# A seventh place for expert pieces, an earlier expert order, and sums moved ahead of the last pair in a two-layer mixture-of-experts decoder kernel

## What is computed

```python
def _hier_moe(u, rg_w, rg_b, re_w, re_b, w1, w3, w2):
    g_prob = softmax(t @ rg_w + rg_b)             # 4 groups of 4 experts
    g_val, g_idx = lax.top_k(g_prob, 1)
    e_prob = softmax(logits of that group)
    e_val, e_idx = lax.top_k(e_prob, EXPERT_TOPK) # 2 experts of the group
    weights = g_val * e_val / sum(e_val)
    h1, h3 = t @ w1[e], t @ w3[e]                 # 16 experts, 1024 x 512 each
    act = silu(h1) * h3 * combine
    return sum over experts of act @ w2[e]        # 512 x 1024
```

## Time and profile before

| what | value |
|---|---|
| time, median of 3 runs | 1069.71 us (1064.26 to 1069.83) |
| the profiled execution, its own time | 1063.24 us |
| its span | 1061.4 us |
| granted TensorE clock, mean share | 0.967 |
| PE busy | 978.4 us (92%) |
| DVE, ACT, POOL busy | 324.4, 174.5, 40.0 us |
| moved by DMA | 316.22 MB, mean 298 GB/s |

### The profile page before, as it was taken

How to read it: one execution, slowest core, us unless ns; L and a number is a source line. 1 busy time by engine, 2 the same in 40 slices (tenths; PEclk the granted TensorE clock), 3 DMA queues, 4 the chain that set the end, 5 groups by cost and what they waited for, 6 DMA issues and landing times.

```text
span 1061.4 us, 13346 instructions
## 1 busy us (share of the span) xinstructions
PE 978.4 (92%) x5418; PEld 552.4 (52%) x5418; DVE 324.4 (31%) x823; ACT 174.5 (16%) x388; POOL 40.0 (4%) x68
## 2 busy tenths in 40 slices
PE   7999999999799989999889798999989998889796
PEld 3666655584464654444443256777664444434353
DVE  3141134216442361111110027738561111111025
ACT  2200000003230231111110012054231111001112
POOL 0000000002210000000002000000000000001000
PEclk9999999979889999999999899999999999999999
DMA  9845777828980529999999984214727999999971
GB/s 379 358 159 199 278 274 284 334 84 325 400 339 5 237 87 418 424 421 422 422 422 421 388 361 160 105 55 175 306 80 309 421 421 423 421 421 422 381 325 50
DMA packets 47622, 316.22 MB, mean 298 GB/s; under 512 B 5602, under 2 KB 6002, under 8 KB 12354
## 3 DMA queue, kind: packets, MB, share of 16 engines
q1 hardware_dynamic: 39456, 288.90, 67.4%
q0 software_dynamic: 6096, 22.30, 5.5%
q10 hardware_dynamic: 2002, 4.08, 1.0%
HBM read 303.84 MB, written 11.42 MB: 297 GB/s over the span
## 4 chain that ended last, share of the span: by engine, by line
PE 65%; DMA 28%; DVE 4%; issue 1%; SPq 1%; ACT 0%; DVEq 0%
PE banks L783 24%; DMA scr<-in_ew 19%; PE banks L1380 8%; DMA ring<-in_ew 6%; PE banks L860 4%; DMA ring<-in_w 3%; PE banks L1347 3%; PE banks L1396 3%; PE banks L1427 3%; PE banks L900 2%; PE banks L1445 1%; PE banks L847 1%; PE banks L1359 1%; PE banks L969 1%; PE banks L1467 1%; PE banks L792 1%
## 5 line engine op out<-in xcount | busy, mean ns | idle before, releaser
L1380 PE MATMUL banks<-scr 128*64 128x512 f32 x448 | 105.6, 621 | 24.7 <-DMA scr<-in_ew 24.4
L783 PE MATMUL banks<-uT,ring 128*128 128x320 f32 x448 | 123.0, 434 | 2.6 <-DVE uT L1629 2.6
L783 PEld LDWEIGHTS banks<-uT,ring 128*128 128x128 f32 x448 | 84.5, 190 | 41.6 <-issue 6.8
L1427 PE MATMUL banks<-ring,scr 128*64 128x512 f32 x448 | 99.7, 596 | 2.9 <-DMA ring<-in_ew 2.9
L1347 PEld LDWEIGHTS banks<-scr 128*128 128x128 f32 x768 | 88.1, 192 | 12.4 <-issue 12.4
L1347 PE MATMUL banks<-scr 128*128 128x128 f32 x768 | 92.1, 277 | 0.0
L1380 PE MATMUL banks<-ring,scr 128*64 128x512 f32 x384 | 84.5, 592 | 0.0
L1380 PEld LDWEIGHTS banks<-scr 128*64 128x64 f32 x448 | 31.9, 141 | 97.6 <-issue 57.6
L594 ACT ACTIVATE scr<-banks,mods 128x128 f32<-128x128 f32 x128 | 36.6, 368 | 204.8 <-PE banks L1347 204.8
L1427 PEld LDWEIGHTS banks<-ring,scr 128*64 128x64 f32 x448 | 30.8, 137 | 60.9 <-issue 54.8
L783 PE MATMUL banks<-ring,uT 128*128 128x512 f32 x128 | 57.0, 598 | 0.0
(11 more groups left out here) (378 smaller groups left out, 1024.7 us busy)
## 6 DMA issues: line engine op xcount, KB each, us to landing
ring<-in_ew SPq DMA_DIRECT2D x128, 1024.0 KB, 20.3
ring<-in_w SPq DMA_DIRECT2D x80, 1024.0 KB, 8.2
scr<-in_ew SPq DMA_DIRECT2D x64, 1024.0 KB, 23.3
yd<-scr POOLq DMA_DIRECT2D x12, 512.0 KB, 8.2
scr<-in_v POOLq DMA_DIRECT2D x16, 256.0 KB, 8.3
scr<-in_kT POOLq DMA_DIRECT2D x13, 256.0 KB, 7.8
out_hgrn<-scr SPq DMA_DIRECT2D x1, 2304.0 KB, 17.8
scr<-in_s POOLq DMA_DIRECT2D x1, 2048.0 KB, 9.5
```

The costliest lines, as they stand in the source:

```text
L783: last = mm(out, a, b, start=(first and i == 0), stop=(final and i == len(pairs) - 1))
L1380: ins = mm(ps[bank][SLOTS * x:SLOTS * x + SLOTS, :], xe[:, kk, SLOTS * x:SLOTS * x + SLOTS], wab[SLOT[n]][:, x, kk % 4, :], start=(kk == 0 ...
L1427: ins = mm(ps[5 + c][SLOTS * x:SLOTS * x + SLOTS, :], actT[:, f, SLOTS * x:SLOTS * x + SLOTS], wab2[SLOT[n]][:, x, f % 2, 512 * c:512 * c ...
```

## The change

1. A place 6 is made in the scratch tile at 10888 (`SPARE`). It lay under `yrows1` before; `yrows1` is now the tile `utok`, the token rows that the pairs' gathers read. So GpSimd waits, ahead of the six indirect DMAs, for the last pair's gather on TensorE (`xe_ps` 16). Some tiles of the dense path, which this input doesn't take, move too.
2. The expert pieces take seven places in a cycle of twelve: with a, b, c, d the ring tiles, a b 4 5 c d 6 a b 4 5 c. Pieces 7 to 11 follow their predecessor in a place at a distance of 7, pieces 12 to 16 at 5, pieces 17 and 18 at 12, and so on every twelve.
3. VectorE makes `order_i` first, with each exchange on 5 of the 8 rows (`swaps[:, TT:, :]`), then `over_i`, the weights, and the exchanges on the other 3 rows. `over_ready` is 2l+1 for the order and 2l+2 for `over_i`; SyncE waits for the first, the others for the second.
4. SyncE's pieces 2 to 5 of layer 0 also wait for `bias_ev` 4.
5. `add_first(6)` goes ahead of `hidden_last` with w1. It takes four products that need only columns 0 to 511 before it waits for ScalarE's copy.
6. In pairs 6 and 7 the second half of the w2 products has c outside, and each half of the columns has its own count, so that VectorE's copy can start when its half is done. `add_last` starts with products of that half. `SUM_ORDER` becomes 0 to 7.

```diff
-    order = further(order[0:2] + [4, 5] + order[2:4], MOE_PIECES)
+    def experts(order):
+        return order[0:2] + [4, 5] + order[2:4] + [6] + order[0:2] + [4, 5] + order[2:3]
+    order = [x for x in further(experts(order), MOE_PIECES) if x < RING]
...
+        SPARE = 10888
+        ring.append(scr[:, SPARE:SPARE + PIECE])
...
-        yrows1 = carve(11392, TT, D)
+        yrows1 = utok
...
-        SUM_ORDER = (0, 4, 1, 5, 2, 6, 3, 7)
+        SUM_ORDER = (0, 1, 2, 3, 4, 5, 6, 7)
...
-                            sp.wait_ge(sem("over_ready"), 2 * l + 2)
+                            sp.wait_ge(sem("over_ready"), 2 * l + 1)
...
-            experts(0, (("res0_ps", 1), ("kv_stored", 64)))
+            experts(0, (("res0_ps", 1), ("kv_stored", 64), ("bias_ev", 4)))
...
                     pool.wait_ge(sem(f"moved{b}"), 16 * stored(l, b, STORED))
+                pool.wait_ge(sem(f"xe_ps{l}"), 2 * NPAIR)
                 for t in ROWS_ORDER:
...
+                def steps(q, h):
+                    f = (2 * h, 2 * h + 1)
+                    if q >= STORED and h == 1:
+                        return [(i, c) for c in range(2) for i in f]
+                    return [(i, c) for i in f for c in range(2)]
...
                 def add_first(q):
                     pe.wait_ge(sem(f"ye_evv{l}"), q + 1)
+                    pe.wait_ge(sem(f"back_ev{l}"), 2)
+                    pe.wait_ge(sem(f"xe_ev{l}"), 2 * NPAIR)
+                    for i in range(4):
+                        prompt(i)
                     pe.wait_ge(sem(f"ye_eva{l}"), q + 1)
...
+                        if m == 4:
+                            pe.wait_ge(sem(f"ye_eva{l}"), q + 1)
...
+                add_first(NPAIR - 2)
                 hidden_last(0, 2, "h1_ps")
-                add_first(NPAIR - 2)
                 hidden_last(1, 3, "h3_ps")
...
+                places = ((NE - 2, MAX, swap), (NE - 1, MIN, swap2))
+                for h, best, oh in places:
+                    step(v.tensor_reduce(key_best, key[:, 2:NE], AX, best))
+                    step(ts(oh, key, key_best, None, EQ))
+                    exchange(swaps[:, TT:, :], h, oh)
+                cp(order_i[0:1, :], swaps[0:1, 2 * TT, 0:NE]).then_inc(sem("over_ready"), 1)
```

More of the change, by code:

```diff
@@ L340, in build @@
         yrows0 = [rows_flat[0][:, 0:D], rows_flat[0][:, D:2 * D], rows_flat[1][:, 0:D]]
[L341 removed]
+        yrows1 = utok
         cdiag = carve(704, 2, TT, P)
[L344 to L346 removed]
+        cb = carve(7424, 2, T)
+        sig = carve(8064, 2, T)
+        rms_all = carve(8704, T)
+        act = rows_flat[0].rearrange("p (a b c) -> p a b c", a=2, b=FT)
         def shift(s):
@@ L1305, in dense @@
                     give(mm(ps[7][:, 0:1], ones[:, :], ones[:, 0:1], start=True, stop=True))
+                mm(ps[7][:, 0:1], ones[:, :], ones[:, 0:1], start=True, stop=True).then_inc(sem(f"xe_ps{l}"), 2 * NPAIR - 3)
             def tokens(l, n):
@@ L1423, in outputs @@
                                 pe.wait_ge(sem(f"ye_eva{l}"), q)
[L1424 to L1430, removed]
+                        for f, c in steps(q, h):
+                            for x in range(2):
+                                ins = mm(ps[5 + c][SLOTS * x:SLOTS * x + SLOTS, :], actT[:, f, SLOTS * x:SLOTS * x + SLOTS],
+                                         wab2[SLOT[n]][:, x, f % 2, 512 * c:512 * c + 512],
+                                         start=(f == 0), stop=(f == FT - 1))
+                                give(ins, f"ye_ps{l}" if f == FT - 1 and (c == 1 or q >= STORED) and x == 1 else None)
                         used(n)
@@ L1440, in outputs_last @@
                             pe.wait_ge(sem(f"actT_ev{l}"), q + 1)
[L1441 to L1447, removed]
+                        for f, c in steps(q, h):
+                            w = wab2[SLOT[n]][:, :, f % 2, 512 * c:512 * c + 512]
+                            for b in range(4):
+                                ins = mm(ps[2 + c][BLOCK * b:BLOCK * b + BLOCK, :], actT[:, f, BLOCK * b:BLOCK * b + BLOCK],
+                                         of_block(w, b), start=(f == 0), stop=(f == FT - 1))
+                                give(ins, f"ye_ps{l}" if f == FT - 1 and b == 3 else None)
                         used(n)
@@ L1739, in slots, with exchange @@
                 counts = ps[6][:, TT * NE:TT * NE + NE]
+                def exchange(rows, h, oh):
+                    n = rows.shape[1]
+                    step(tt(change[:, 0:n, :], rows[:, :, h:h + 1].broadcast_to([P, n, NE]), rows[:, :, 0:NE], SUB))
+                    step(tt(change[:, 0:n, :], change[:, 0:n, :], over(oh, n, 1), MUL))
+                    v.tensor_reduce(total[:, 0:n].unsqueeze(2), change[:, 0:n, :], AX, ADD)
+                    step(tt(rows[:, :, 0:NE], rows[:, :, 0:NE], change[:, 0:n, :], ADD))
+                    step(tt(rows[:, :, h:h + 1], rows[:, :, h:h + 1], total[:, 0:n].unsqueeze(2), SUB))
+                ts(swaps[:, 2 * TT, 0:NE], const[:, K_IOTA:K_IOTA + NE], -NOWHERE, None, ADD)
+                step(stt(key, counts, float(NE), const[:, K_IOTA:K_IOTA + NE], MUL, ADD))
+                places = ((NE - 2, MAX, swap), (NE - 1, MIN, swap2))
[4 more added lines that the diff above has]
+                cp(order_i[0:1, :], swaps[0:1, 2 * TT, 0:NE]).then_inc(sem("over_ready"), 1)
                 v.tensor_reduce(n_most, counts[:, 2:NE], AX, MAX)
@@ L1749, in slots @@
                 step(v.tensor_reduce(n_over, fits[:, 32:36], AX, MAX))
+                ts(split_i[0:1, 0:1], n_most[0:1, :], float(SLOTS), None, ALU.is_le)
                 ts(over_i[0:1, 0:1], n_over[0:1, :], 0.0, None, MAX).then_inc(sem("over_ready"), 1)
[L1751 to L1753 removed]
                 combine(l)
[L1756 to L1764 removed]
+                for h, _, oh in places:
+                    exchange(swaps[:, 0:TT, :], h, oh)
                 ts(kept, slot[:, :, 0:NROWS], NOWHERE, None, GE)
```

66 lines of the change are left out of this document (33 added, 33 removed).

## The result

The changed kernel takes 1059.48 us at the median of 9 runs (1058.75 to 1062.91), the kernel before 1067.48 in 9 runs (1060.49 to 1070.01). The ratio is 0.9946, 95% interval 0.992 to 0.9971. It is faster, since the interval leaves out 1, by 5.8 us in 1067.5 by this ratio, which goes by the means (the medians lie 8.0 us apart), where 16 were forecast. The profiled execution took 1061.77 us, 1.5 less than the one before.

What follows compares the result with a forecast made beforehand. The two expert stages were taken as bound by the DMA queue, with a TensorE tail. Gains of 7.5 + 7.0 + 1.6 = 16.1 us gave 1047.1 from the profiled execution, 1053.6 from the median; 1051 was named, range 1044 to 1061.

Steps and rivals of the forecast that it cites:

- Part 1: Seventh place: piece 6 loads in the empty queue stretch before the expert stage, 4.2 us of shift kept a layer.
- No bubble: At piece 12 of the expert stream: data flows from 425.0 us, queue free at 425.7, 0.7 us to spare.
- Bubble 0.8 us: At piece 15: data flows from 441.5 us, queue free at 440.6, so 0.8 us of the shift is lost.
- Shift lost: Rival, 0.10: distances of 5 give back all 4.98 us, piece 45 lands as before; 1055.5 us, 1062.0 on the median.
- Part 2: `order_i` made first on VectorE: order 3 us earlier, near 385.5 us; booked 0, bounds 0 to 1 us a layer.
- Part 4: `add_first` ahead of the last pair fills TensorE's idle time; h3 ends 7.5 and 7.0 us earlier, behind piece 45.
- A piece takes TensorE 3.5 us: At the last w3 piece: TensorE's time for one piece, from 7.09 us for two, sets the end of h3.
- the clock rival: Rival, 0.12: idling before the last w3 piece drops TensorE's clock, costing 4.4 us; 1051.5 us, 1055 to 1058 on the median.
- Part 6: GpSimd waits before the six gathers: rows land near 609.5 us, 6 us to spare before `turn_rows`; booked zero.
- Part 5: Halves of the last w2 products: the 0.77 us wait between `outputs_last` and `add_last` goes, 0.8 us a layer.
- 7.25: Earlier end of h3 a layer, forecast as 7.5 us in layer 0 and 7.0 in layer 1.

Runs made afterwards that it cites:

- The rotation without short distances: Changed kernel with the expert pieces in plain rotation through seven places, every distance 7, dense path not kept right: 1055.41 us, 0.9888 to the kernel before.
- the last experiment: Plain rotation of seven with four gathers early, and the expert order put last again behind `over_i`, weights and other exchanges: 1056.85 us, 0.9918 to the kernel before.
- the extra matmuls: Plain rotation of seven plus four unused 128x512 matmuls between the last pair's two w3 pieces: 1055.53 us, 0.9876; with four gathers early too, 1057.73 us, 0.9913.
- early gathers: Four of six gathers go out before GpSimd's wait: on the plain rotation 1053.75 us, on the changed kernel 1058.18, with distances of 6 1056.5.
- 4.4 by the second: The changed kernel run once more, unedited, for a second profile: 1060.22 us, ratio 0.9959 to the kernel before.

## Why the prediction was wrong

1. **The direction and the outline of the mechanism were right.** Piece 6 is loaded into the empty stretch (2.2 MB in 16 us). `add_first` fills the idle time ahead of h1. The end hangs on piece 45, as the sum had it.
2. **Part 1, the shift of 4.2 us, is the first term that failed.** Piece 45 came 0.3, 0.4, 3.7 and 2.4 us earlier behind the start than in the kernel before, in the two profiles' layers: 1.7 on average (about 2 between the means over all profiles with six places and with the cycle of twelve). The step in error is "No bubble" at piece 12 and "Bubble 0.8 us" at piece 15. I took the latency into an empty queue, 2.4 us, for the lead that a full queue needs. Measured, leads of 3.1 and 3.3 us cost 1.7 and 2.1 us. My own rows gave a lead of 3.1 us at piece 12, which is what it had, and 1.5 at piece 15. The rotation without short distances gave 3.4 and 4.9 us against the kernel before. "Shift lost" stood among the rivals with 0.10.
3. **Part 2, the early order at 0, isn't refuted.** The order came 4.9 us earlier against the start of `hidden_first`, not 3. The late order of the last experiment costs 2 us a layer, but it is later than the order of the kernel before, with which I had compared; how much of the 2 us belongs to the term is open.
4. **Part 4 held up to piece 45, and failed behind it.** "A piece takes TensorE 3.5 us" was right only with the clock up. The last w3 piece took 6.10 and 5.23 us. This is the clock rival, at 0.12; it was in nearly every stage with all gathers late: without the extra matmuls, h3 ended 5.4 to 6.7 us behind piece 45 in 11 of 12 layers, and 3.7 to 3.8 us behind it in all ten layers of the five kernels that have early gathers or GpSimd's old order beside the moved sums, again without the extra matmuls. It was the likeliest case, not a rival. The cost is 2.4 us a layer. The Trainium skill's warning ("TensorE: Matmul & The Clock Gate", HAM oscillation) was the better guide here: in all eleven of these waits of 3.7 us and more for the last w3 piece the work behind was slow.
5. **Part 6, GpSimd's wait at nothing, missed its real price.** I had checked that the rows come in time, and they do, though the first gather went out at 588.1 us and the last landed at 615.2, not at 582.5 and 609.5. What I didn't follow is that the gathers' bytes now lie between pieces 42 and 45, make their landings 7.4 to 9.8 us apart, and so make the wait that drops the clock. The same wait also brings pieces 40 to 42 forward; alone it made the kernel before faster, by 0.4%.
6. **Part 5 was right:** 0.8 us, the gap of 0.77 to 0.81 us is gone from every trace with the halves.
7. Worked again with these sizes, h3 ends 7.25 - 2.5 (shift 1.7 instead of 4.2) - 2.4 (clock) = 2.35 us earlier a layer. With 0.8 that is 3.15 a layer, 6.3 in all; measured are 5.8 by the first ratio and 4.4 by the second. That the sum fits so well is partly luck, since single profiles of one kernel differ by 2 to 3 us at piece 45.

What stays open: in layer 0 TensorE stood idle 1.5 to 1.9 us between its look at `over_i` and the first product behind it in five of the eleven profiled executions with the seventh place, 1.2 to 1.5 us in layer 1 of three of them, and never over 0.4 in the three kernels without it. Its cause is open; where it is over 1 us, piece 7 is issued 9.6 to 10.3 us behind the start of `hidden_first`, and 8.1 to 8.8 in the other stages with the seventh place. And why one lead of 2.9 us and one of 2.6 cost nothing, where 3.1 cost 1.7 us, isn't settled.

## What to carry to other kernels

A further buffer is worth its size only if every later transfer keeps its lead: list, for each transfer, when it can be issued and when the one ahead of it lands, and ask for the lead that held the stream full (here 5 us), not for the latency into an empty queue. When a transfer is moved beside others, ask not only whether it comes in time, but what it does to the spacing of the others, and whether the longest wait that this makes on TensorE is long enough to drop its clock. For this input, a rotation that uses each place in turn beat a cycle with the same number of places and the same mean distance by 0.6%; it leaves the dense path out. And when an experiment puts an old order back, read from its trace that it is back where it was, not later.

## What the runs showed of the hardware

- A DMA queue that is about to run dry loses rate before it is empty. From 441 to 449 us it moved 317 GB/s at a busy share of 0.93, while piece 14 was still landing until 444.3 us, and the halves of piece 15 landed 4.0 and 4.4 us behind the half ahead of them instead of 2.5.
- Ahead of the last w3 piece, TensorE's eleven waits of 3.7 to 6.2 us were each followed by a slow piece (5.2 to 6.6 us instead of 3.64), and its eleven waits of 1.2 to 1.8 us by none, extra matmuls left aside. It is no rule for the whole stage: behind waits of 2.0 to 2.3 us both occur, and in three of the stages with short waits the clock fell later, under `outputs_last` (8.7 to 8.8 us instead of 7.07).
- The spread between executions of one kernel goes with the clock. The fastest of all executions of the kernel before took 1054.9 us at a mean granted clock of 0.980 and the slowest 1071.1 at 0.960, the others roughly in that order. The profile before lay at 0.967 and showed the clock at 1.00 from 379 to 395 us; 12 of the 13 later profiles show 0.79 to 0.94 there.
